# Hybrid encoder kernel: the score of the next tile between the two half-turns of a step, VectorE's score passes behind them, new keys split a step ahead

## The reference: what is computed

```python
def hybrid_layer(x, g, w_in, w_out, lq1, lk1, lq2, lk2, subln_g, rpb, lam_init):
    h = rms_norm(x, g)
    z = jnp.einsum('bsd,de->bse', h, w_in)
    qd, kd, vd, qn, kn, vn, gate = jnp.split(z, cuts, axis=-1)
    ...
    o_da = diff_attention(qd, kd, vd, lam, lam_init, subln_g)
    ...
    o_na = neighbourhood_attention(qn, kn, vn, rpb)
    o = jnp.concatenate([o_da, o_na], axis=-1) * jax.nn.silu(gate)
    return x + jnp.einsum('bse,ed->bsd', o, w_out)
```

## Time and profile before

| | us |
|---|---|
| median of 3 runs | 1486.92 (1486.36 to 1487.51) |
| the profiled execution | 1487.66 |
| its span, first to last instruction | 1485.9 |

### The profile page before, as it was taken

How to read it: one execution, slowest core, us unless ns; L and a number is a source line. 1 busy time by engine, 2 the same in 40 slices (tenths; PEclk the granted TensorE clock), 3 DMA queues, 4 the chain that set the end, 5 groups by cost and what they waited for, 6 DMA issues and landing times.

```text
span 1485.9 us, 23642 instructions
## 1 busy us (share of the span) xinstructions
PE 1434.3 (97%) x8160; PEld 1168.9 (79%) x8160; DVE 877.3 (59%) x1814; ACT 684.4 (46%) x1306; POOL 492.0 (33%) x384
## 2 busy tenths in 40 slices
PE   7999999999999999999999999999999999999994
PEld 6788787878788888777887878788788888887874
DVE  6666676666656565743436666766665565656423
ACT  5445454445444444652524444545454544456330
POOL 2323223133333333443643132322233333336261
PEclk9999999999999999999999999999999999999997
DMA  4700101112021111301110111000202020203112
GB/s 177 148 29 22 49 21 35 35 36 61 29 61 43 53 43 54 128 29 56 58 43 29 37 36 35 21 28 21 75 22 75 22 74 21 75 29 128 43 44 113
DMA packets 39258, 79.57 MB, mean 54 GB/s; under 512 B 18832, under 2 KB 18832, under 8 KB 39184
## 3 DMA queue, kind: packets, MB, share of 16 engines
q1 hardware_dynamic: 39184, 78.60, 16.6%
HBM read 66.57 MB, written 15.96 MB: 56 GB/s over the span
## 4 chain that ended last, share of the span: by engine, by line
PE 89%; DVE 3%; ACT 2%; issue 2%; SPq 2%; DMA 1%; POOL 0%; DVEq 0%; POOLq 0%; ACTq 0%
PE proj L956 19%; PE proj L958 17%; PE proj L957 17%; PE scores L992 10%; PE turn L1049 5%; PE mix L1101 3%; PE mix L1102 3%; PE mix L1066 2%; PE mix L1065 2%; PE mix L1067 2%; PE scores L1049 2%; SPq L485 2%; PE mix L1075 1%; ACT prob L815 1%; DVE pt_lo L1394 1%
## 5 line engine op out<-in xcount | busy, mean ns | idle before, releaser
L956 PE MATMUL proj<-h_hi,w_hi 128*128 128x512 f32 x1184 | 500.9, 423 | 11.5 <-DVE h_lo L1295 10.3
L958 PE MATMUL proj<-h_hi,w_lo 128*128 128x512 f32 x1184 | 466.3, 394 | 0.0
L957 PE MATMUL proj<-h_lo,w_hi 128*128 128x512 f32 x1184 | 463.4, 391 | 0.0
L956 PEld LDWEIGHTS proj<-h_hi,w_hi 128*128 128x128 f32 x1184 | 223.1, 188 | 75.4 <-issue 35.5
L958 PEld LDWEIGHTS proj<-h_hi,w_lo 128*128 128x128 f32 x1184 | 222.5, 188 | 51.6
L586 POOL TENSOR_TENSOR w_lo<-w_raw,w_hi 128x1024 fp32r<-128x1024 f32 x78 | 191.8, 2459 | 199.3 <-ACT w_hi L748 199.3
L957 PEld LDWEIGHTS proj<-h_lo,w_hi 128*128 128x128 f32 x1184 | 224.0, 189 | 33.9
L1386 DVE CUSTOM_DVE_ANT_0 prob<-scores,inner 128x1024 f32<-128x1024 f32 (+1 forms) x192 | 204.0, 1062 | 70.7 <-PE scores L992 69.9
L1394 DVE TENSOR_TENSOR pt_lo<-turn,pt_hi 128x512 fp32r<-128x512 f32 x208 | 139.2, 669 | 155.0 <-ACT pt_hi L790 153.5
L790 ACT ACTIVATE pt_hi<-turn 128x512 fp32r<-128x512 f32 x208 | 120.5, 579 | 222.4 <-PE turn L1049 221.7
L815 ACT ACTIVATE prob<-prob,nm,escale_now 128x1024 f32<-128x1024 f32 x128 | 158.1, 1235 | 3.3 <-DVE nm L1390 3.2
(11 more groups left out here) (162 smaller groups left out, 2268.2 us busy)
## 6 DMA issues: line engine op xcount, KB each, us to landing
w_raw<-chunks SPq DMA_DIRECT2D x81, 512.0 KB, 3.5
mixed_dram<-gate SPq DMA_DIRECT2D x28, 256.0 KB, 2.0
edge<-bias_dram SPq DMA_DIRECT2D x32, 224.0 KB, 3.9
h_lo<-mixed_dram SPq DMA_DIRECT2D x14, 512.0 KB, 6.9
xt<-x_t SPq DMA_DIRECT2D x8, 512.0 KB, 9.5
bias_dram<-bias_rows SPq DMA_DIRECT2D x16, 240.0 KB, 6.1
out_t<-prob SPq DMA_DIRECT2D x6, 512.0 KB, 3.0
out_t<-gate SPq DMA_DIRECT2D x2, 512.0 KB, 3.0
```

The source lines that it names most:

```text
L956: pe.matmul(dst, a_hi, b_hi, start=start, stop=False)
L957: pe.matmul(dst, a_hi, b_lo, start=False, stop=False)
L958: return pe.matmul(dst, a_lo, b_hi, start=False, stop=stop)
```

## The change

`score` of tile t+1 (in step 7: tile 0 of the group behind) is issued in step t, between fill 1 and the second half-turn, instead of at the head of step t+1; step 8 has none there, and `score(behind, 1)` stays at its end. `sum_pair` moves behind fill 0, `spread_factor` from the end of odd steps to behind fill 0 of the next even step. The fills are cut 3, 2, 3 instead of 2, 3, 3 (in step 8 still 2, 3, 3; in step 1 behind a DA group 1, 2, 1 instead of 1, 3, 0; before the last group 1, 2, 1 instead of 1, 1, 2). VectorE: `combine` moves ahead of the second subtraction, the score passes of tile t+1 come behind the subtractions and ahead of `piece_part`; `k_lo_part` goes to the head of step 7; tile 1's passes of the group behind come last in step 8. ScalarE: each exponential goes ahead of the copy of its half-turn, `mean_square` behind the first exponential, `k_hi_part` to step 6 behind the copies.

```diff
-    GATE_HEAD = [range(0, 1), range(1, 2), range(2, 4)]
+    GATE_HEAD = [range(0, 1), range(1, 3), range(3, 4)]
...
+        def following(g, behind, t):
+            if t < NT - 1:
+                return g, t + 1
+            return (behind, 0) if t == NT - 1 and behind else None
...
# ScalarE, attend
-                    if g.project and t == NT - 1:
-                        k_hi_part(g)
                     if front and ft == 0:
                         begin_group(front)
-                    if not g.na and t % 2 and t >= 3:
-                        mean_square(g, (t - 3) // 2)
                     rows = ROWS_HI[t] if not behind and t in ROWS_HI else [[]] * 3
                     for c in range(2):
+                        if front:
+                            exponentials(front, ft, c)
+                        if c == 0 and not g.na and t % 2 and t >= 3:
+                            mean_square(g, (t - 3) // 2)
                         p_part(g, t - 1, c)
                         for i in rows[0] if c == 0 else []:
                             take_mixed(g.l, i)
-                        if front:
-                            exponentials(front, ft, c)
                     if g.na and INNER[t - 1]:
                         p_part(g, t - 1, 2)
+                    if g.project and t == NT - 2:
+                        k_hi_part(g)
...
# TensorE, step
-                if front and ft != 1:
-                    score(front, ft)
-                parts = [range(0, 2), range(2, 5), range(5, 8)]
+                parts = [range(0, 3), range(3, 5), range(5, 8)]
+                if t == NT:
+                    parts = [range(0, 2), range(2, 5), range(5, 8)]
                 if t == 1 and not (ended and ended.na):
-                    parts = [range(4, 5), range(5, 8), ()]
-                if not g.na and t % 2 and t >= 3:
-                    sum_pair(g, (t - 3) // 2)
+                    parts = [range(4, 5), range(5, 7), range(7, 8)]
...
                 fill(0)
+                if not g.na and t % 2 and t >= 3:
+                    sum_pair(g, (t - 3) // 2)
+                if not g.na and t % 2 == 0 and t >= 4:
+                    spread_factor(g, t // 2 - 2)
                 turn_p(g, t - 1, 0)
                 fill(1)
+                if following(g, behind, t):
+                    score(*following(g, behind, t))
                 turn_p(g, t - 1, 1)
...
-                elif not g.na and t >= 3:
-                    spread_factor(g, (t - 3) // 2)
...
# VectorE, step
-                if front:
+                def shift_scores(g, t):
                     for m in range(2):
-                        shifted(front, ft, m)
+                        shifted(g, t, m)
...
+                if g.project and t == NT - 1:
+                    k_lo_part(g.group() + 1)
                 for c in range(3 if g.na and INNER[t - 1] else 2):
                     if c < 2:
                         add_pieces(c)
                     p_part(g, t - 1, c)
                     if c == 0 and not g.na and t % 2 == 0 and t >= 4:
                         gated(g, t // 2 - 2)
+                    if c == 0 and front:
+                        combine(front, ft)
                     if c == 0 and ended and not ended.na:
                         gated(ended, PAIRS - 1)
-                    if g.project and t == NT - 1 and c == 0:
-                        k_lo_part(g.group() + 1)
-                if front:
-                    combine(front, ft)
+                if following(g, behind, t):
+                    shift_scores(*following(g, behind, t))
                 if not g.project:
                     if t in GATE_FILL:
                         piece_part(g, t - 1)
...
+                if t == NT and behind:
+                    shift_scores(behind, 1)
...
                 piece_part(g, 0)
+                for c in range(2):
+                    shifted(g, 1, c)
                 from_second(dve, l, step)
```

## The result

The changed kernel takes 1556.42 us (median of 4 runs, 1554.36 to 1558.41) against 1486.64 us: ratio 1.0469, interval 1.0451 to 1.0487, so 69.8 us slower. Forecast were 1532 us, range 1508 to 1554. The sign and the kind of waits were right, the size was too small by 24 us, and the time lies 2.4 us above the range. The profiled execution took 1554.36 us, its span is 1552.6, its mean granted clock 0.975 (0.992 before).

What follows compares the result with a forecast made beforehand. TensorE, near 97% busy, bounds the kernel, so its waits and operand changes decide. Waits sum to +45.1 us, operands -3, clock +3: 1487.66 + 45 = 1532.7, 1532 on the median's level; range 1508 to 1554.

Steps and rivals of the forecast that it cites:

- Waits of the turns: Second half-turns: DA step 8 +22.5 us, DA-to-NA +2.3, NA-to-NA +4.5, before last groups +4.8, step 2 +7.5.
- What stands behind the turn: Delay from the late turn to the weighing: 0.6 us in DA step 8, 0.3 in step 2.
- the chain of the forecast: VectorE's piece pass, ScalarE's q copy or tanh, w_hi, exponential, copy of the turn, then VectorE's subtraction release the turn.
- Clock: TensorE's clock falls behind some long waits at 1.5 us each; two falls taken, +3 us.
- the 22 waits of the forecast: TensorE's new long waits, some of which may each cost 1.5 us more through the clock.
- Rival (a): Clock falls at most boundaries, 14 of 22 waits or more: 1550 to 1562 us; chance 0.13.
- Last groups: Each layer's last group, step 2: tanh and exponential ahead of the copies hold the weighing; +2.5 us for both layers.
- Change of operand: TensorE's scores are now left into a turn: saves 12 us at most, taken as -3.
- Costs taken at nothing: Score banks, moved sums, keys' split and later store in step 1: zero, between -1 and +3 us in sum.
- (b): Chain only half as late, only DA step 8 pays, at its lower bound: 1504 to 1515 us; chance 0.17.
- (d): The gain in step 2 (combine) pays for the loss: 1484 to 1490 us; chance 0.02.
- (c): Faster: the score between half-turns covers the one-bank round trip, nothing comes late: 1465 us; chance 0.08.

Runs made afterwards that it cites:

- the run with both edits: Changed kernel plus 12 unread matmuls ahead of the second turn in steps 2 and 8, and VectorE's combine behind the second subtraction there: 1534.17 us (1.0339).
- the run with the unread matmuls alone: Changed kernel plus 12 matmuls nobody reads, ahead of the second turn of steps 2 and 8 where both groups are DA: 1549.76 us (1.0434).

## Why the prediction was too low, point by point

- **Waits of the turns: right.** From start to start, less the usual distance, the step 8 turn waits 3.27 us at each of six DA boundaries (forecast 3.2), 1.25 at DA to NA (1.1), 1.19 at NA to NA (1.1), 2.51 before the last group (2.5); step 2 waits 2.8 to 3.6 (3.0). The chain that sets them was the right one: shortening it at either end won 39 us.
- **What stands behind the turn: the first step that failed.** The forecast had 0.6 us (step 8) and 0.3 (step 2) until the weighing. Weighing starts show what it was, for the group of the earlier trace rows and the next weighing. After the change:

```profile
208.99 0.28 PE L1072 MATMUL mix<-pt_hi,v_hl 128*128 128x256 f32 x1
...
231.94 0.28 PE L1072 MATMUL mix<-pt_hi,v_hl 128*128 128x256 f32 x1
...
259.05 0.28 PE L1072 MATMUL mix<-pt_hi,v_hl 128*128 128x256 f32 x1
```

With the clock kept up and the combine late (the run with both edits):

```profile
202.72 0.28 PE L1072 MATMUL mix<-pt_hi,v_hl 128*128 128x256 f32 x1
...
224.08 0.28 PE L1072 MATMUL mix<-pt_hi,v_hl 128*128 128x256 f32 x1
...
249.76 0.28 PE L1072 MATMUL mix<-pt_hi,v_hl 128*128 128x256 f32 x1
```

  22.95 and 27.11 us against 21.36 and 25.68: 1.6 and 1.4 behind each wait, not 0.6 and 0.3. Over 14 DA steps that is some 15 us more than the forecast, and the run with both edits, which has the waits still but not this, is 20 us below the changed kernel. The two steps fail for different reasons, and the run with the unread matmuls alone tells them apart, for it has the clock up and the combine where the change put it. Its step 8 takes 21.90 us, 0.5 to 0.6 over 21.36: the chain of the forecast was right there, and the rest is the clock. The changed kernel's own boundaries agree: 21.96 us at the one without a stretch at 1.2 GHz, 22.6 to 23.0 at three with one, 23.5 at the two with the long one. Its step 2 takes 27.0 us, 1.4 over 25.6 (the median of the other run's), with the clock up: there the chain was priced at 0.3 and is 1.4, since the small scale operation of the combine stands behind GpSimd's w_lo for 1.27 us instead of 0.22 (255.58 above). The slow matmuls of step 2 lie beside it and cost as much, so that neither edit alone shortened it.
- **Clock: size wrong, and the mechanism half right.** I took two falls; the trace has 15, 13 of them at the 22 waits of the forecast and two at a wait that it did not have. The 2.7 us wait that kept the clock misled me as evidence. The stretch shown there ends just behind the wait; the next one has the clock up too:

```profile
75.00:158.00 83.00, 81.12 (x482) 65.67 (x482) 56.60 (x107) 41.73 (x82) 21.13 (x18) 1.00 0.10 33
```

  But it was one case: in the changed kernel waits of 2.5 to 3.6 us are followed by the lower level in 15 of 18 places. The Trainium skill (TensorE: Matmul & The Clock Gate, "HAM oscillation") has idle gaps take the clock down; the trace agrees for waits of this size, with 15 falls. The price of a fall, 1.5 us in the forecast, holds where nothing lies beside it (1.6 at the waits of the scores). Behind the turns it is covered in part: filling the waits won 4 us, since the combine's chain lay beside them.
- **Rival (a)** gave the right time, 1550 to 1562 us, with nearly the right number of falls, and partly by luck: it prices 12 more falls at 1.5 each on top of the forecast, while in step 2 they cost what the mispriced chain costs anyway, and the last groups, which it does not have, bring 12 us.
- **Last groups: the second step that failed.** Forecast +2.5 for both layers, measured 6.03 + 8.09 = 14.1. I followed ScalarE's tanh and exponential in step 2 and did not ask what else stands behind the moved score passes: the addition to the residual rows. A stretch at 1.2 GHz behind that wait belongs to it. The two layers are alike in the changed kernel; the 2.1 us between 6.03 and 8.09 are mostly the fall that the kernel before has in layer 0 alone. Reordering these groups alone won 9 us by the times.
- **Change of operand: right sign, too small.** Between two undisturbed weighings the time fell. Before, then after:

```profile
263.36 0.28 PE L1065 MATMUL mix<-pt_hi,v_hl 128*128 128x256 f32 x1
...
283.27 0.28 PE L1065 MATMUL mix<-pt_hi,v_hl 128*128 128x256 f32 x1
```

```profile
278.79 0.28 PE L1072 MATMUL mix<-pt_hi,v_hl 128*128 128x256 f32 x1
...
298.57 0.28 PE L1072 MATMUL mix<-pt_hi,v_hl 128*128 128x256 f32 x1
```

  19.91 to 19.78 us here, and 0.12 to 0.25 in most DA pairs that no wait or slow stretch touches; I take 0.14. Single pairs of NA groups say less, for other tiles' scores, of other sizes, now stand in them (some pairs grew by 0.2). A whole NA group, from weighing to weighing, grew from 73.48 to 74.26 us with a wait of 1.19 in it, which leaves a gain of 0.10 a pair. For the 56 pairs outside the last groups this is an estimate of 7 us, where the forecast took 3 of at most 12.
- **Sum.** 45 forecast, + 15 behind the turns, - 3 as the clock's term is in them, + 12 for the last groups, - 4 for the operands: 65, against 66.7 between the two spans. Some 2 us are not placed.
- **Costs taken at nothing.** In ordinary steps nothing waits for the score banks or the keys, as forecast. The keys' split ahead is what makes that so: undone, it costs 22.5 us. The later store in step 1 cost the changed kernel nothing, but only because the score passes covered it.
- **Rivals (b) to (d)** fell: no boundary was half as late, and ordinary steps' slack did not reach step 8. What (c) had hoped for is in the change all the same: with the engines' orders mended it runs at 1467.93 us.

## What to carry to other kernels

When work moves earlier on one engine, list everything that then stands behind it in the other engines' written orders, at the boundaries and in the last group above all: the ordinary step gained slack here, and the boundary steps and last groups lost some 70 us in sum. Put first what hands a PSUM bank back to TensorE (copy, subtraction, addition), then what it needs only a step later (exponentials, score passes, combine). Price a late operation up to the next point where engines meet, and not at its first wait only: behind a wait of 3 us another 1.5 us was lost, in step 2 to two causes of which either hid the other. A moved operation also meets other work of the engines that it had not met before, as the combine met GpSimd's w_lo.

## What the runs showed of the hardware

The granted clock fell to 1.2 GHz in or right behind waits of 2.5 to 3.6 us in 15 of 18 places, and a wait of 2.7 us in the kernel before left it at 2.4, so that the size of the wait alone does not tell. A fall cost 1.6 us where nothing lay beside it, at the waits of the scores. A fall costs less than its slow matmuls suggest where another engine's chain ends as late: with the falls of the DA boundaries gone the kernel won 4 us, and 20 once that chain was shorter too.

A VectorE operation of 0.22 us on one number per partition, with operands in SBUF alone, lasted until GpSimd's operation was over whenever it started during one: ten of ten in the changed kernel, up to 3.18 us, each ending 0.02 us behind GpSimd, and none of the other 54. Not every VectorE operation does so: the subtraction L1403, which reads PSUM, kept its 0.69 us beside GpSimd.
